# Gate matrix of an expert layer: compare against column numbers in PSUM, three row scalings on GpSimd and one on ScalarE

## What is computed

```python
q = (xb @ wq).reshape(nt, 8, 2, 128)
s = einsum('thcd,hckd->thck', q, subkeys)          # two score lists of 128 keys per head
s1, i1 = top_k(s[:, :, 0], 16);  s2, i2 = top_k(s[:, :, 1], 16)
top_s, pos = top_k(all sums s1 + s2, 16)           # 16 of 256 pairs
idx  = i1[...] * 128 + i2[...]                     # expert = (row, column) of a 128 x 128 grid
gate = softmax(top_s)
act  = gelu(einsum('thkd,td->thk', u_tab[idx], xb)) * gate
y    = einsum('thk,thkd->td', act, v_tab[idx])
```

## Time and profile before

| | us |
|---|---|
| median of three runs | 4235.46 |
| the profiled execution's own time | 4235.86 |
| its span, first to last instruction | 4234.1 |
| TensorE matmul busy | 3680.3 |
| VectorE busy | 3221.9 |
| GpSimd busy | 2074.4 |
| ScalarE busy | 1264.6 |

### The profile page before, as it was taken

The page is one execution under the profiler, slowest core; times in us unless marked ns, Lnnn a source line. Parts: engine busy times, 40 slices in busy tenths (PEclk is TensorE's granted clock), DMA queues, the critical chain, the costliest instruction groups (busy, mean ns, idle before and its releaser), DMA issues. The chain is left out here.

```text
span 4234.1 us, 51468 instructions
## 1 busy us (share of the span) xinstructions
PE 3680.3 (87%) x17523; PEld 2894.4 (68%) x17523; DVE 3221.9 (76%) x5977; ACT 1264.6 (30%) x2010; POOL 2074.4 (49%) x1349
## 2 busy tenths in 40 slices
PE   6985579896779999999997957894779999999997
PEld 2454355443669989988986546452668998998996
DVE  1036554577979999999998167298979999999998
ACT  1031131111743333333332133101743333333332
POOL 0000000134967767777875000034966777778775
PEclk8987689898989999999998955997989999999999
DMA  4410001341579999999997100111569999999997
GB/s 199 163 43 6 0 1 40 130 170 51 159 233 396 396 398 400 391 405 401 398 397 307 67 23 1 50 40 40 158 221 394 397 398 399 398 401 402 398 396 304
DMA packets 318724, 1013.09 MB, mean 239 GB/s; under 512 B 23351, under 2 KB 121655, under 8 KB 296089
## 3 DMA queue, kind: packets, MB, share of 16 engines
q0 software_dynamic: 149936, 546.03, 33.1%
q1 hardware_dynamic: 166882, 440.55, 27.5%
q10 hardware_dynamic: 1800, 25.24, 1.6%
HBM read 958.16 MB, written 53.56 MB: 239 GB/s over the span
## 5 line engine op out<-in xcount | busy, mean ns | idle before, releaser
L1331 POOL DMA_INDIRECT arena<-in_peer_v,picked x512 | 834.1, 1629 | 238.5 <-issue 122.5
L1331 POOL DMA_INDIRECT arena<-in_peer_u_rows,picked x512 | 765.2, 1495 | 346.5 <-DVE dots L1924 220.4
L831 PE MATMUL pair<-h_hi,u_hi 128*128 128x384 f32 x2048 | 689.5, 337 | 30.9 <-issue 30.9
L831 PE MATMUL pair<-h_lo,u_hi 128*128 128x384 f32 x2048 | 687.5, 336 | 0.0
L831 PE MATMUL pair<-h_hi,u_lo 128*128 128x384 f32 x2048 | 687.2, 336 | 0.0
L1944 DVE SCALAR_TENSOR_TENSOR gate<-arena,act,gate 128x1024 f32<-128x1024 f32 x512 | 640.7, 1279 | 6.7 <-DVE act L1936 6.6
L1924 DVE CUSTOM_DVE_ANT_0 arena<-arena 128x1024 f32<-128x1024 f32 x512 | 612.3, 1219 | 15.1 <-DVE dots L1930 15.1
L831 PEld LDWEIGHTS pair<-h_hi,u_hi 128*128 128x128 f32 x2048 | 387.5, 189 | 40.0 <-issue 34.3
L1108 ACT ACTIVATE u_hi<-ring 128x2048 fp32r<-128x2048 f32 x128 | 245.5, 1919 | 519.5 <-DMA ring<-in_peer_u 519.4
L831 PEld LDWEIGHTS pair<-h_lo,u_hi 128*128 128x128 f32 x2048 | 387.4, 189 | 6.4
L831 PEld LDWEIGHTS pair<-h_hi,u_lo 128*128 128x128 f32 x2048 | 387.1, 189 | 0.0
(11 more groups left out here) (300 smaller groups left out, 5810.5 us busy)
## 6 DMA issues: line engine op xcount, KB each, us to landing
ring<-in_peer_u SPq DMA_DIRECT2D x128, 1024.0 KB, 8.0
ring<-in_peer_v SPq DMA_DIRECT2D x128, 1024.0 KB, 9.3
routing<-arena SPq DMA_DIRECT2D x24, 2048.0 KB, 8.7
arena<-routing SPq DMA_DIRECT2D x64, 768.0 KB, 9.8
ring<-in_w_ada SPq DMA_DIRECT2D x12, 2048.0 KB, 10.2
ring<-in_w_ada ACTq DMA_DIRECT2D x12, 2048.0 KB, 7.8
ring<-in_peer_wq SPq DMA_DIRECT2D x8, 2048.0 KB, 7.9
ring<-in_w_in SPq DMA_DIRECT2D x6, 2048.0 KB, 12.9
```

What stands on the lines that cost most here:

```text
L831: last = mm(pair[:, j, 0:TD], R(u[b][:, P * (KD * j + k):P * (KD * j + k + 1)]), R(h[:, k, :]), start=(k == 0 and i == 0), stop=(k == KD - ...
L1331: pool.indirect_dma_start(gathered[:, b, :], None, rows, bass.IndirectOffsetOnAxis(picked[:, n:n + 1], 0)).then_inc(sem[f"row_in{b}"], 16)
```

## The change

The column and row numbers 0 to 127 are copied once per layer from SBUF into the first 128 elements of PSUM bank 1, and VectorE's compare reads them there instead of in SBUF. GpSimd's product takes three of a job's four row one-hots instead of two, and ScalarE scales one instead of two.

```diff
@@ ScalarE, routing_matrix, scale_hots @@
-                            for q in range(2):
-                                ins = do(hots[:, m % 4, 0, q, :], hots[:, m % 4, 0, q, :], ACT.Copy,
-                                         scale=cols[:, b, 2, 4 * n + q:4 * n + q + 1])
-                            ins.then_inc(sem["gated_a"], 1)
+                            do(hots[:, m % 4, 0, 0, :], hots[:, m % 4, 0, 0, :], ACT.Copy,
+                               scale=cols[:, b, 2, 4 * n:4 * n + 1]).then_inc(sem["gated_a"], 1)
@@ GpSimd, routing_matrix @@
-                            rows = hots[:, m % 4, 0, 2:4, :]
-                            nc.gpsimd.tensor_tensor(rows, rows, bc(cols[:, b, 2, 4 * n + 2:4 * n + 4], P, 2),
+                            rows = hots[:, m % 4, 0, 1:4, :]
+                            nc.gpsimd.tensor_tensor(rows, rows, bc(cols[:, b, 2, 4 * n + 1:4 * n + 4], P, 2),
                                                     ALU.mult).then_inc(sem["gated_p"], 1)
@@ VectorE, routing_matrix @@
             def routing_matrix(l):
+                link(V.tensor_copy(bank[1][:, 0:P], iota))
                 jobs = TB // 4
@@
                             tt(hots[:, m % 4], bc(cols[:, b, 0:2, 4 * n:4 * n + 4], P, 3),
-                               bc(bc(iota, 4, 1), 2, 1), ALU.is_equal).then_inc(sem["hot_ready"], 1)
+                               bc(bc(bank[1][:, 0:P], 4, 1), 2, 1), ALU.is_equal).then_inc(sem["hot_ready"], 1)
```

## The result

The changed kernel takes 4165.44 us, the median of four runs (4161.44 to 4169.97), against 4237.14 for the kernel before: a ratio of 0.9834, with a 95% interval of 0.9820 to 0.9848. That is 72 us less, where 60 were forecast. The profiled execution took 4161.74 us, with a span of 4159.9 against 4234.1.

The account below looks back on a forecast made before the run. DVE's compare and POOL's product colliding, 0.41 us a job, bound the gate stage. 2 x (11 x 2.9 + 0.3 - 0.2) = 64.0, less 4.4 for clock falls, is 59.6; 4235.9 - 59.6 = 4176.3; range 4160 to 4200, chance 0.74.

Parts of the forecast that it names:

- (a): DVE's compare alone, column numbers in PSUM: no price difference from SBUF, 1.14 us per job.
- Rival B: Reading PSUM costs DVE's compare more: 0.05 us each gives 4185, an estimated 65 ns gives 4187; chance 0.05.
- (b): Whether POOL's product still gets in the compare's way: 0 us per job taken, against 0.41 before.
- POOL's third row: POOL's product over three rows takes 0.82 us, hidden by the next job's compare except at a layer's end.
- Copy of the numbers: One more DVE instruction per layer, some 0.4 us, hidden ahead of a 2.51 us wait; without cover 0.8 us.
- Blocks: Eight gate-stage jobs on DVE, which still sets the pace: from 12.42 to 9.5 us, 2.9 gained each.
- C: Next limit, PE or the longest transfer, makes blocks 9.9 or 10.0 us: 9 to 11 us, 4184 to 4186; chance 0.09.
- 0.9 us a job on PE: Lower figure for PE's gate-stage job, from 25 matmuls in 2.60 us; upper figure 1.11.
- the transfer's 9.0 a block: Block's transfer to memory, 8.7 us plus 0.28 until issue, limits each block to 9.0 us, 10.0 at the longest.
- the clock's: Falls of PE's clock in three blocks, three jobs each at 0.57 us: 5.1 less 0.7, so 4.4 us off.
- The first blocks: Each layer's first block, held by the ACT chain, gains only 0.3 us, from ACT's dropped scaling.
- the tail: A layer's last POOL product, no compare behind it, is on the path: 0.2 us a layer lost.

Follow-up runs that it names:

- run 2: Changed kernel with the column numbers copied to another SBUF tile instead of PSUM; 4276.13 us, ratio 1.0093.
- run 4: Kernel before without POOL's products: ACT scales all four rows, both compare inputs in SBUF; 4257.31 us in a single execution.
- run 3: Kernel before with the compare's other input, the picks' places, copied to PSUM once per block, column numbers in SBUF; 4168.04 us, ratio 0.9834.
- run 7: Changed kernel with the compare cut to its row half, column one-hots not made (not a usable version); 4152.9 us in a single execution.
- run 1: Changed kernel with the scalings put back to two rows each on POOL and ACT, column numbers in PSUM; 4169.73 us, ratio 0.9836.
- run 8: The changed kernel measured once more, unaltered, for comparison on one chip; 4169.32 us, ratio 0.9845 to the kernel before.
- run 5: Changed kernel with POOL scaling all four rows and ACT none; 4160.88 us, ratio 0.9822 to the kernel before.

## Why the prediction was right, and where its size was off

The time lies in the range, and the mechanism is the one forecast; run 2 against the changed kernel shows it with only the place of the numbers different, and run 4 with POOL's product taken away.

- *Price of the compare* (a): 1.14 taken, 1.13 measured from start to start. Rival B falls: 1210 to 1223 ns from PSUM against 1217 to 1227 from SBUF in run 4.
- *Collisions* (b): 0 taken; the spread of 13 ns leaves none. The Trainium skill's rule in SBUF — State Buffer, "Who interferes with whom", holds here in both parts that were used, a collision with two SBUF inputs and none with one, whichever input it is (run 3).
- *POOL's third row*: 826 ns, 0.82 taken. *Copy of the numbers*: hidden, as DVE still waits 2.74 us behind the first four compares.
- *Blocks*: 9.5 taken, 9.43 measured. *C* did not come in the changed kernel: transfer and PE stay just below DVE. Two of its terms were wrong in size all the same. The row given for 0.9 us a job on PE, 25 matmuls in 2.60 us, makes 0.83; run 7 has 7.41 us for eight, 0.93 each. And the transfer's 9.0 a block holds in every second block alone (run 7), its longest time only for the first of a layer (run 1). C's 9 to 11 us on 4176 make 4185 to 4187, not 4184 to 4186.
- *The sum* is where the size was off. From the first compare of a layer to h_hi the two stages gained 69 us (330.9 to 261.9, and 261.5 in run 8) against 59.6. The term that was mis-sized most is the clock's: 4.4 us taken off for three falls, and neither this profile nor run 8's has one in a steady block. This profile's:

```profile
1057.40:1166.00 108.60, 94.30 (x722) 84.79 (x720) 104.61 (x101) 81.26 (x180) 77.25 (x90) 1.00 0.76 213
2930.00:3036.00 106.00, 93.21 (x716) 83.96 (x715) 104.56 (x101) 80.90 (x180) 74.92 (x89) 1.00 0.78 218
```

(Windows, columns as above: the granted clock, third from the end, is 1.00 over all steady blocks of either layer.) What failed is the count, not so much the price. A fall was put at three jobs and 1.71 us; the row given shows only two jobs at half speed, 16 matmuls in 3.68 us, but the blocks with a fall in runs 1 and 3 were 1.38, 1.96 and 1.70 us longer than the others, ACT's wait for a transfer included in the last two. The first blocks gained 1.5 and 0.8 us against 0.3 each (+1.7), the steady ones 0.09 a block more (+2), and the tail, from the start of the last compare, for which 0.2 a layer was taken off, gave 0.6 and 0.3 (+1.3); 0.4 of each is that compare itself. POOL's last product was not the free one that the 0.2 assumes: DVE's split held it before too, at 2657 ns, the maximum in the earlier trace rows, and at 2807 now. 59.6 + 4.4 + 1.7 + 2 + 1.3 = 69.0.
- The other 5 us between the two profiled spans lie outside the stages. The first compare starts 2.4 us sooner though nothing ahead of it changed but the copy of the numbers, which is one instruction more; over these profiles it starts anywhere from 1042.3 to 1049.5. As far as these runs show, that is their spread and no part of the change: run 8's median is 64.7 us under the kernel before, its stages gained as much as here.
- The scalings' new division adds nothing that the times can tell (4165.44 and, in run 8, 4169.32, against 4169.73 in run 1). By the traces the two stages take 261.9 and 261.5 us against 264.5, and run 1's two long third blocks are more than that difference. In the profile it shortens PE's pause at a block's end, and it opened the way to run 5.

## What to carry to other kernels

When two engines show the same mean time per job and a minimum far below the median, suspect that they hold each other up, and price the collision by the instruction's minimum. Here moving one small constant input of a two-input VectorE instruction to a free PSUM bank took the collision away at no price that the profile shows, and moving the other input did so for 0.14 us a block. Before giving more work to the engine that collides, take the collision away first: the same third row cost 39 us with it and nothing without.

## What the runs showed of the hardware

- A collision costs less than the whole of POOL's product: 1.55 - 1.14 = 0.41 us of 0.61 with two rows, 1.765 - 1.135 = 0.63 of 0.83 with three (run 2). In both, a job is 0.2 us shorter than compare and product one behind the other.
- A two-input compare that reads the same 128 elements of PSUM eight times over runs as fast as from SBUF, at 1024 elements in 1.21 us.
- TensorE's granted clock fell to 0.50, the 1.2 GHz level, for 3 us and more at a time, and what sets a fall is left open. In run 1 it fell soon after PE had stood for 1.59 us at a block's end, and this is the stretch, in a window:

```profile
1076.00:1079.00 3.00, 3.00 (x16) 3.00 (x16) 2.18 (x2) 1.94 (x6) 1.16 (x3) 0.50 1.07 292
```

In the steady blocks of the changed kernel, with pauses of 1.05 to 1.13, there was none. But run 4, whose PE stood for 1.93 us at a block's end and 0.49 ahead of most other jobs, kept 1.00 over its steady blocks, so the longest pause does not decide it, and run 7 kept 1.00 through pauses of 1.65 from its fourth block on. The five falls of runs 1, 3 and 7 in a steady block are all in the third block of a layer, behind a pause of 1.59 to 2.84 us in which ACT waited 0.13 to 1.67 us for the layer's first transfer; whether that wait matters to the clock is not shown. In the kernel before, a fourth block, 1061.1 to 1073.6, stood at 0.86 as well; the prediction counted three.
